# A hybrid two-layer decoder trunk: logarithms, scans and the second mixer's preparation moved to earlier places

## The chip, the cores and the metric

The kernel runs on one core of one Trainium2 chip. The metric is the device time of one execution in microseconds (us). Engines: TensorE (PE) multiplies, VectorE (DVE) and ScalarE (ACT) do elementwise work, SyncE (SP) issues the DMAs. Each engine works through its own instructions in order and waits on semaphores.

## The reference, cut to what matters

Two layers over 256 tokens of width 1024, all float32:

```python
h = rmsnorm(x); p = h @ W_in            # 3592 columns, four head groups
A = hgrn2(...)        # gated linear recurrence, 4 heads x 64, log_f = log of a gate, cumulated
B = gated_deltanet(...)  # conv, l2norm, (I + lower)^-1 by chunks
C = rglru(...)        # associative scan over 256 channels
D = rwkv7(...)        # generalised delta state update
x = x + concat(A, B, C, D) @ W_out
x = x + cross_attention(rmsnorm(x), rmsnorm(mem))     # 256 memory tokens, keys and values from mem
x = x + swiglu(rmsnorm(x))              # layer 0; layer 1: top 2 of 8 experts
```

## The kernel before, in words

Activations stay in SBUF. A weight chunk of 1 MB (128 x 2048 floats) comes by DMA into one of three `raw` buffers; ACT rounds it to `whi` (L447), DVE makes the rest `wlo = raw - whi` (L871, L1318), and PE multiplies in three passes (hi*hi, lo*hi, hi*lo). `plan_chunks` lists the order of loads, and the ring of three `raw` buffers means that load d starts when chunk d - 3 is used up. `ahead(n)` on ACT and DVE splits chunks up to n at that point of the engine's program.

A layer runs so:

1. Input projection: 14 chunks, `cm_phase` on PE, evacuated by ACT (`cm_evac`) with a hook `gates_ahead(l, j)` ahead of chunk j on each engine.
2. `gates(l)` and `logs(l)`: lora products, sigmoids, the logarithms of the decays.
3. `hgrn(l)`: the cumulated decay by four scans, then LEVELS = 7 levels. At level v ACT makes an exponential, DVE two products `H` ("hg_qk"), PE the scores, DVE takes them over (`take`) and makes the differences of level v + 2 (`diff`). Between these stand steps of the RG-LRU (`rglru(l, v)`). Behind the levels: the state, the outputs and the preparation of the delta mixer (norms of q and k, decays `gd_cum`, `rel`).
4. `deltanet(l)`: a triangular inverse in seven levels (`inverse`, DVE and PE in turn, "first inverse" here), with parts of RWKV between, then a tail of two solves, a state and the outputs. On DVE it is preceded by `head_out`, the gated norm of the HGRN output.
5. `rwkv(l)`: masks, a second `inverse`, a tail, then the first products with `w_out`.
6. `attention(l)`: norm, query product, scores, output product.

The keys and values of the memory do not depend on x. Their eight pieces `kv(l, i)` of 16 products each (plain float32, straight out of `raw`) are spread over steps 3 to 5 on PE as filler; `KV_BANK` gives their PSUM banks and `kv_put` their evacuation by ACT. A `w_out` part on PE is `tm_part`, and `tm_add` on DVE adds the result to x.

Of the kernel before, what the change touches and what calls it, by code (L numbers as in the profile page):

```python
# [14 lines left out]
P = 128  # L15
D = 1024
# [6 lines left out]
NH = 4  # L23
# [59 lines left out]
def plan_chunks():  # L83

    out = []
    for layer in range(DEPTH):
        out += [("cm", "w_in", layer, c) for c in W_IN_COLS]
        out += [("tm", "w_out", layer, TM_ROWS * j) for j in range(3)]
        out += [("kv", "xattn_wk", layer, c) for c in range(0, D, CM_COLS)]
        out += [("kv", "xattn_wv", layer, c) for c in range(0, D, CM_COLS)]  # L90
        out += [("tm", "w_out", layer, 3 * TM_ROWS)]
        out += [("cm", "xattn_wq", layer, c) for c in range(0, D, CM_COLS)]
        out += [("tm", "xattn_wo", layer, r) for r in range(0, KT, TM_ROWS)]
        if layer == 0:
            steps = D_FF // CM_COLS
            for j in range(steps + 1):
                if j < steps:
                    out += [("cm", "ffn_w_gate", 0, CM_COLS * j), ("cm", "ffn_w_up", 0, CM_COLS * j)]
                if j:
                    out += [("tm", "ffn_w_down", 0, TM_ROWS * (j - 1))]  # L100
    return out


def build(nc, A, out):
# [14 lines left out]
    with ExitStack() as ctx:  # L119
# [14 lines left out]
        x = sb("x", TT * D)[:, :].rearrange("p (t n) -> p t n", t=TT)  # L134
        hT = [sb(f"hT_{s}", KT * SEQ, F32R)[:, :].rearrange("p (c n) -> p c n", c=KT) for s in ("hi", "lo")]
        def shared(name, cols, before, dt=F32):
            return nc.alloc_sbuf_tensor_at(name, [P, cols], dt, offset=nc.sbuf_base - before)

        hE_flat = [sb(f"hE_{s}", KT * SEQ, F32R) for s in ("hi", "lo")]
# [100 lines left out]
        G_N = H(7), H(13)  # L240
# [120 lines left out]
        KV_BANK = [7, 5, 6, 7, 6, 7, 7, 2]  # L361
# [67 lines left out]
        def _(act):  # L429
# [35 lines left out]
            def cm_evac(n0, count, dst, scale=1.0, after=None):  # L465
                for j in range(count):
# [3 lines left out]
                    ahead(n + SPL)  # L470
# [15 lines left out]
            def kv_put(l, i):  # L486

                bank, j = KV_BANK[i], i % NH
# [6 lines left out]
            def gates_ahead(l, j):  # L495
# [17 lines left out]
                if j == 11:  # L513
                    act.wait_ge(S("shift"), l + 1)
                    a(PT[0:64, D_W * SEQ:(D_W + 1) * SEQ], PT[0:64, D_W * SEQ:(D_W + 1) * SEQ], ACT.Tanh)
                    a(pt(D_G, 1), pt(D_G, 1), ACT.Sigmoid).then_inc(S("lora_in"), 1)
                    a(tmp(0), pt(A_F), ACT.Sigmoid, scale=-1.0).then_inc(S("s_kA"), 1)
                    a(tmp(1), pt(A_G), ACT.Sigmoid)
                if j == 12:
                    a(tmp(2), pt(B_Z), ACT.Sigmoid).then_inc(S("s_z"), 1)  # L520
                    if l:
                        a(tmp(5), pt(A_F), ACT.Sigmoid)
                if j == 13:
                    act.wait_ge(S("gelu_in"), l + 1)
                    a(tmp(4), tmp(4), ACT.Sigmoid).then_inc(S("gelu_s"), 1)

            def gates(l):

                ahead(first_chunk["w_out", l] + SPL)
                act.wait_ge(S("lora_mm"), l + 1)  # L530
                for j in range(2):
                    a(pt(C_X)[:, 256 * j:256 * j + 256], ps[:, 2, 256 * j:256 * j + 256], ACT.Sigmoid, bias=pc("rwkv_w0", l, j))
                for j in range(2):
                    a(pt(D_W)[:, 256 * j:256 * j + 256], ps[:, 3, 256 * j:256 * j + 256], ACT.Sigmoid, bias=pc("rwkv_a0", l, j))
                a(H(12), ps[:, 4, :], ACT.Copy).then_inc(S("lora_s"), 1)
                if l:
                    act.wait_ge(S("vmix_mm"), 1)
                    a(H(13)[0:32, 0:256], ps[0:32, 5, 0:256], ACT.Copy).then_inc(S("vmix1"), 1)
                    act.wait_ge(S("vmix_mm"), 2)
                    for j in range(2):  # L540
                        a(tmp(3)[:, 256 * j:256 * j + 256], ps[:, 6, 256 * j:256 * j + 256], ACT.Sigmoid,
                          bias=pc("rwkv_v0", None, j)).then_inc(S("vmix2"), 1)

            def logs(l):

                o, o2 = PCOL["gdn_A_log", l][0], PCOL["lru_lambda", l][0]
                table("exp_and_others")
                act.wait_ge(S("gd_x"), l + 1)
                a(col(ST_SP, 8), col(ST_X, 8), ACT.Abs)
                a(col(ST_LAM, 2), par[:, o2:o2 + 2], ACT.Abs)  # L550
                if l == 0:
                    a(tmp(5), pt(A_F), ACT.Abs)
                    a(tmp(5), tmp(5), ACT.Exp, scale=-1.0)
                a(col(ST_SP, 8), col(ST_SP, 8), ACT.Exp, scale=-1.0)
                a(col(ST_EXPA, 4), par[:, o:o + 4], ACT.Exp)
                a(col(ST_LAM, 2), col(ST_LAM, 2), ACT.Exp, scale=-1.0)
                if l == 0:
                    a(tmp(5), tmp(5), ACT.Ln, bias=1.0).then_inc(S("hg_ln"), 1)
                else:
# [3 lines left out]
                a(col(ST_LAM, 2), col(ST_LAM, 2), ACT.Ln, bias=1.0).then_inc(S("lam_sp"), 1)  # L563
                table("exp_and_others")

            def rglru(l, v):

                if v == 1:
                    act.wait_ge(S("lru_log"), l + 1)
                    a(H(10), H(8), ACT.Exp)  # L570
                    a(H(11), H(8), ACT.Exp, scale=2.0).then_inc(S("lru_a"), 1)
                if v == LEVELS - 1:
                    act.wait_ge(S("lru_gain"), l + 1)
                    a(G_N[0], pt(B_Q), ACT.Square)
                    a(G_N[1], pt(B_K), ACT.Square).then_inc(S("gd_sq"), 1)

            def hgrn(l):
                for v in range(LEVELS):
# [5 lines left out]
                    if v % 2 == 0 and v < LEVELS - 1:  # L584
                        kv_put(l, v // 2)
                    rglru(l, v)
                act.wait_ge(S("hg_qk"), (l + 1) * LEVELS)
                a(tmp(6), pt(A_F), ACT.Exp)
                for c in range(2):
                    b = pt(A_F)[:, 256 * c:256 * c + P]  # L590
                    a(tmp(7)[:, P * c:P * c + P], b, ACT.Exp, scale=-1.0, bias=b[:, P - 1:P]).then_inc(S("hg_end"), 1)
                table("natural_log")
                a(H(11), H(11), ACT.Ln)
                kv_put(l, 3)
                act.wait_ge(S("gd_ss"), l + 1)
                for j in range(2):
                    a(G_N[j], ps[:, j, :], ACT.Ln, bias=epsc(0))
                act.wait_ge(S("hg_trk"), l + 1)
                a(tmp(5)[:, 0:256], ps[:, 5, 0:256], ACT.Copy).then_inc(S("hg_kd"), 1)
                a(H(11), H(11), ACT.Exp, scale=0.5).then_inc(S("lru_root"), 1)  # L600
                for j in range(2):
                    a(G_N[j], G_N[j], ACT.Exp, scale=-0.5).then_inc(S("gd_rn"), 1)
                act.wait_ge(S("gd_gd"), l + 1)
                a(col(ST_GD, 8), col(ST_GD, 8), ACT.Exp)
                act.wait_ge(S("gd_cum"), 3 * l + 3)
                a(tmp(2), ps[:, 4, :], ACT.Exp).then_inc(S("gd_eg"), 1)
                for p_ in range(2):
# [1702 lines left out]
```

## Time and profile before

| | us |
|---|---|
| median of 3 runs | 1986.95 (1986.77 to 1990.31) |
| the profiled execution | 1990.8 |
| its span | 1989.0 |
| PE busy | 1873.3 (94%) |
| DVE busy | 1466.7 (74%) |
| ACT busy | 1131.7 (57%) |

The share of busy time is an average over stages with different limits. The mixers (steps 2 to 5) of layer 0 lie between 109 and 288 us, those of layer 1 between 675 and 857 us; the experts fill the time from 975 us to the end.

### The profile page before, as it was taken

The page shows a single profiled execution, that of the slowest core. Times are in us where ns is not written, and L with a number is a line of the kernel's source. Part 1 is how long each engine was busy: PE and PEld are TensorE (multiplying, and loading weights), DVE is VectorE, ACT ScalarE, POOL GpSimd, SP SyncE. Part 2 cuts the span into 40 slices and gives each one's busy share as a digit, 9 for nine tenths or more (in the row PEclk, how much of TensorE's full clock was granted, in tenths as well). Part 3 has the DMA queues.
Part 4 walks back from the last instruction along what each step waited for, and adds up shares of the span by engine and source line. Part 5 has one row for each costly group of instructions (what it writes and reads, how often), then busy time and mean ns, then how long its engine had stood idle before and what let it go on. Part 6 is the DMA issues. An engine that isn't in the chain of part 4 may idle for free.

```text
span 1989.0 us, 29716 instructions
## 1 busy us (share of the span) xinstructions
PE 1873.3 (94%) x12520; PEld 1617.3 (81%) x12521; DVE 1466.7 (74%) x1547; ACT 1131.7 (57%) x1065; POOL 0.2 (0%) x4
## 2 busy tenths in 40 slices
PE   7998799999999988899699999999999999999996
PEld 6976688899989877778588888888888888888885
DVE  6767645444457677553698989989899898998985
ACT  5555224443344652143377767777677777777774
POOL 0000000000000000000000000000000000000000
PEclk9998899999999999899799999999999999999998
DMA  7541004255545421023499999999999999999992
GB/s 239 171 149 59 28 23 162 85 191 182 182 145 170 157 78 44 23 92 118 161 345 341 381 345 366 370 330 379 346 369 367 330 380 346 370 365 333 377 374 97
DMA packets 239450, 465.99 MB, mean 234 GB/s; under 512 B 11856, under 2 KB 87760, under 8 KB 239312
## 3 DMA queue, kind: packets, MB, share of 16 engines
q1 hardware_dynamic: 239312, 464.03, 65.6%
q8 instruction: 101, 1.65, 0.3%
q14 instruction: 37, 0.30, 0.0%
HBM read 462.95 MB, written 1.05 MB: 233 GB/s over the span
## 4 chain that ended last, share of the span: by engine, by line
PE 84%; DVE 10%; ACT 3%; issue 2%; DMA 0%; DVEq 0%; SPq 0%; ACTq 0%
PE ps L2077 31%; PE ps L1557 15%; PE ps L2087 15%; PE ps L1542 11%; PE ps L1577 6%; DVE MT L858 4%; PE ps L2133 2%; PE ps L1622 1%; PE ps L2108 1%; ACT MT L438 1%; DVE MT L861 1%; PE ps L2148 1%; DVE MT L864 1%; DVE x L858 1%; DVE TMP L858 1%
## 5 line engine op out<-in xcount | busy, mean ns | idle before, releaser
L1318 DVE TENSOR_TENSOR wlo<-raw,whi 128x2048 fp32r<-128x2048 f32 x140 | 320.4, 2291 | 55.7 <-ACT whi L736 55.5
L736 ACT ACTIVATE whi<-raw 128x2048 fp32r<-128x2048 f32 x140 | 268.9, 1922 | 120.8 <-PE ps L2087 71.2
L871 DVE TENSOR_TENSOR wlo<-raw,whi 128x2048 fp32r<-128x2048 f32 x85 | 194.5, 2289 | 98.9 <-ACT whi L447 98.7
L1318 DVE TENSOR_TENSOR wlo<-PT,whi 128x2048 fp32r<-128x2048 f32 x84 | 192.1, 2292 | 31.2 <-ACT whi L736 30.2
L447 ACT ACTIVATE whi<-raw 128x2048 fp32r<-128x2048 f32 x85 | 162.1, 1907 | 45.2 <-PE ps L1577 43.6
L2077 PE MATMUL ps<-whi,hE_hi 128*128 128x512 f32 x672 | 185.4, 398 | 2.4 <-DVE hE_lo L1387 2.4
L736 ACT ACTIVATE whi<-PT 128x2048 fp32r<-128x2048 f32 x84 | 161.4, 1922 | 34.9 <-PE ps L2077 34.2
L2077 PE MATMUL ps<-wlo,hE_hi 128*128 128x512 f32 x672 | 180.1, 390 | 0.0
L2077 PE MATMUL ps<-whi,hE_lo 128*128 128x512 f32 x672 | 179.8, 389 | 0.0
L2077 PEld LDWEIGHTS ps<-wlo,hE_hi 128*128 128x128 f32 x672 | 126.2, 188 | 27.2
L2077 PEld LDWEIGHTS ps<-whi,hE_lo 128*128 128x128 f32 x672 | 126.1, 188 | 26.7
L2077 PEld LDWEIGHTS ps<-whi,hE_hi 128*128 128x128 f32 x672 | 122.0, 188 | 24.8 <-DVE hE_lo L1387 2.6
L2087 PE MATMUL ps<-whi,act_hi 128*128 128x512 f32 x336 | 130.8, 389 | 1.4 <-DVE act_lo L1362 1.4
L2087 PE MATMUL ps<-whi,act_lo 128*128 128x512 f32 x336 | 130.8, 389 | 0.0
L2087 PE MATMUL ps<-wlo,act_hi 128*128 128x512 f32 x336 | 130.7, 389 | 0.0
L1542 PE MATMUL ps<-MT 64*64 64x64 f32 (+1 forms) x2528 | 98.9, 233 | 26.4 <-DVE MT L858 18.8
L1542 PEld LDWEIGHTS ps<-MT 64*64 64x64 f32 (+1 forms) x2528 | 90.4, 146 | 38.4 <-issue 19.2
L1557 PE MATMUL ps<-hT_hi,whi 128*128 128x256 f32 x848 | 119.7, 284 | 0.0
L1557 PE MATMUL ps<-hT_hi,wlo 128*128 128x256 f32 x848 | 119.0, 283 | 0.0
L1557 PE MATMUL ps<-hT_lo,whi 128*128 128x256 f32 x848 | 119.0, 283 | 0.0
L858 DVE TENSOR_TENSOR MT<-MT,ps 128x256 f32<-128x256 f32 (+2 forms) x99 | 44.6, 450 | 90.2 <-PE ps L1557 75.5
L1557 PEld LDWEIGHTS ps<-hT_hi,whi 128*128 128x128 f32 x848 | 109.9, 192 | 0.9
(272 smaller groups left out, 3397.5 us busy)
## 6 DMA issues: line engine op xcount, KB each, us to landing
raw<-in_moe_w_up SPq DMA_DIRECT2D x111, 1024.0 KB, 6.8
PT<-in_moe_w_down SPq DMA_DIRECT2D x56, 1024.0 KB, 6.4
PT<-in_moe_w_gate SPq DMA_DIRECT2D x55, 1024.0 KB, 6.7
TMP<-in_moe_w_gate SPq DMA_DIRECT2D x55, 1024.0 KB, 6.6
raw<-in_moe_w_down SPq DMA_DIRECT2D x55, 1024.0 KB, 6.0
raw<-in_w_in SPq DMA_DIRECT2D x28, 1024.0 KB, 5.4
raw<-in_ffn_w_gate SPq DMA_DIRECT2D x11, 1024.0 KB, 5.3
raw<-in_ffn_w_up SPq DMA_DIRECT2D x11, 1024.0 KB, 5.5
```

What stands on the lines that cost most here:

```text
L438: return chain.link(lambda: nc.scalar.activation(o, i, f, **kw))
L447: nc.scalar.activation(whi[i % SPL][:, :], raw[d % RAW][:, :], ACT.Copy).then_inc(S("w_hi"), 1)
L736: nc.scalar.activation(ex_hi[m % XSPL], ex_raw[m % XRAW], ACT.Copy).then_inc(S("w_hi"), 1)
L858: return chain.link(lambda: V.tensor_tensor(o, x0, x1, op))
L871: V.tensor_tensor(wlo[i % SPL][:, :], raw[d % RAW][:, :], whi[i % SPL][:, :].bitcast(F32), ALU.subtract).then_inc(S("w_lo"), 1)
L1318: V.tensor_tensor(ex_lo[m % XSPL], ex_raw[m % XRAW], ex_hi[m % XSPL].bitcast(F32), ALU.subtract).then_inc(S("w_lo"), 1)
L1542: return Signalled(pe.matmul(o, lhsT, rhs, start=start, stop=stop, skip_group_check=True))
L1557: ins = pe.matmul(ps[:, bank, SEQ * m:SEQ * m + SEQ], wp[a_][:, k, P * m:P * m + P], src[b_][:, k, :], start=i == 0 and k == 0, stop=last)
L1577: ins = pe.matmul(ps[:, 4 + 2 * t + hf, :], src(b_, kk, t), wp[a_][:, kk, 512 * hf:512 * hf + 512], start=first and kk == 0 and i == 0, st ...
L2077: ins = pe.matmul(ps[:, bank, :], h_[b_][:, X_K * i + k, :], wp[a_][:, k, :], start=i == 0 and n_ == 0 and k == 0, stop=i == 1 and n_ == 2 ...
L2087: ins = pe.matmul(ps[:, 4 + hf, :], act_[b_][:, P * (TM_ROWS * i + kk):P * (TM_ROWS * i + kk) + P], wp[a_][:, kk, 512 * hf:512 * hf + 512] ...
L2133: ins = pe.matmul(g_tokens(c), xs[:, t, P * c:P * c + P], oneh[:, P * t:P * t + P], start=t == 0, stop=t == 1)
```

## The change

Nothing is computed differently but for the form of one polynomial; work changes its place, and some intermediate results lie in buffers of the weight split (`spare`) that are free in the mixers.

- The lora products, the logarithms, the four scans and the first two differences are hooks of the projection's chunks 10 to 12. So are the products for the norms of the delta mixer's q and k.
- `second(v)` puts the delta mixer's preparation and the HGRN state into the seven levels, on PE and DVE.
- The last RG-LRU step and the HGRN `head_out` stand in levels 4 and 2 of the first inverse.
- The eight `kv` pieces have other places, the last one in `attention`, half of it (PRE = 4 of 8) ahead of the norm; the load order follows.
- The `w_out` chunks 0 to 2 are split in the mixers' tails instead of right behind the projection.
- `tm_add` asks for one split less before it adds; `norm` asks for it.

```diff
@@ plan_chunks
-        out += [("tm", "w_out", layer, TM_ROWS * j) for j in range(3)]
-        out += [("kv", "xattn_wk", layer, c) for c in range(0, D, CM_COLS)]
-        out += [("kv", "xattn_wv", layer, c) for c in range(0, D, CM_COLS)]
-        out += [("tm", "w_out", layer, 3 * TM_ROWS)]
+        out += pieces[0:4] + w_out[0:1] + pieces[4:6] + w_out[1:2] + pieces[6:7] + w_out[2:4] + pieces[7:8]
@@ scalar
-                if j == 11:
+                if j == 10:
...
+                if j == 12:
...
+                    logs(l)
+            def gates_late(l, j):
+                if j != 11:
+                    return
+                act.wait_ge(S("lora_mm"), l + 1)
...
+                a(G_N[0], pt(B_Q), ACT.Square)
+                a(G_N[1], pt(B_K), ACT.Square).then_inc(S("gd_sq"), 1)
@@ vector
+                def second(v):
+                    if v == 0:
...
+                        stt(pt(B_Q), pt(B_Q), HD ** -0.5, G_N[0], ALU.mult, ALU.mult)
+                    if v == 1:
+                        tt(pt(B_K), pt(B_K), G_N[1], ALU.mult)
+                        dve.wait_ge(S("gd_cum"), 4 * l + 2)
+                        tt(g_kb(l), pt(B_K), ps[:, 5, :], ALU.mult).then_inc(S("gd_ops"), 1)
...
+                def beside(v):
+                    rwkv_ahead(l, v)
+                    if v == 2:
+                        head_out(l, 0, 7, tmp(0), lambda c: pc("hgrn_norm", l, c), pt(A_G), 0)
+                    if v == 4:
+                        rglru(l, LEVELS)
+                inverse(2 * l, after=beside)
...
+                ahead(first_chunk["w_out", l] + 1)
@@ tensor
+            def second(l, v):
+                if v == 0:
+                    pe.wait_ge(S("hg_v"), l + 1)
...
+                if v in (2, 3):
...
+                            mm(ps[:, 4, a_:a_ + P], col(k).to_broadcast([P, P]), incl).then_inc(S("gd_cum"), 1 if t and c else 0)
...
-                kv(l, 0, range(KT))
+                kv(l, 0, range(KT // 2))
...
+                    if v < 5:
+                        kv(l, (v + 1) // 2, range(KT // 2) if v % 2 else range(KT // 2, KT))
@@ deltanet, rwkv_ahead(v)
-                    if v < 2:
-                        kv(l, 5, range(KT // 2 * v, KT // 2 * v + KT // 2))
+                    if v >= 3:
+                        pe.wait_ge(S("y_put"), 4 * l + 1)
+                        kv(l, 3, range(2 * v - 6, 2 * v - 4))
@@ rwkv, turn_operands(v)
+                    kv(l, 5, [v, v + 1] if v == LEVELS - 1 else [v])
@@ attention
+                kv(l, 7, range(PRE))
                 pe.wait_ge(S("x_done"), 6 * l + 2)
                 norm(2 + 3 * l)
+                kv(l, 7, range(PRE, KT))
```

PE, layer 0, from the end of the input projection to the second level. The rows with `sw` are the lora products, those with `memT` the `kv` pieces, `64x64` the scores, `128x8` the sums of the delta mixer's decay. Before:

```order
L1542 MATMUL ps<-PT,sw 128x256 x6
L1545 MATMUL ps<-con,PT 128x128 x4
L1542 MATMUL ps<-memT,raw 128x256 x16
L1542 MATMUL ps<-PT,TMP 64x64 x16
L1542 MATMUL ps<-st,con 128x8
L1542 MATMUL ps<-st 128x8
L1542 MATMUL ps<-memT,raw 128x256 x8
L1542 MATMUL ps<-MT 64x64 x16
L1542 MATMUL ps<-memT,raw 128x256 x8
```

The same place in the changed kernel, where line 1602 is the old 1542:

```order
L1605 MATMUL ps<-con,PT 128x128 x4
L1602 MATMUL ps<-PT,TMP 64x64 x16
L1602 MATMUL ps<-memT,raw 128x256 x8
L1602 MATMUL ps<-st,con 128x8
L1602 MATMUL ps<-st 128x8
L1602 MATMUL ps<-MT 64x64 x16
L1602 MATMUL ps<-con,TMP 128x128 x8
L1602 MATMUL ps<-memT,raw 128x256 x8
```

The lora products are gone from here (they stand in the projection), one piece and a half ahead of level 0 became half a piece, and level 0 has eight products of `second`.

DVE, first inverse, levels 2 to 4 of the changed kernel (`ps,con16b` x2 starts a level, `MT<-MT,ps` x4 ends it; `spare_hi_49` are the RG-LRU's tiles):

```order
L907 TENSOR_TENSOR MT<-ps,con16b 128x256 x2
L907 TENSOR_TENSOR TMP<-ps,TMP 128x512
L913 SCALAR_TENSOR_TENSOR TMP<-TMP,par,PT 128x256 x2
L1125 CAST hT_hi<-TMP 128x512
L907 TENSOR_TENSOR hT_lo<-TMP,hT_hi 128x512
L907 TENSOR_TENSOR MT<-MT,ps 128x256 x4
L907 TENSOR_TENSOR MT<-ps,con16b 128x256 x2
L907 TENSOR_TENSOR MT<-MT,PT 128x512 x2
L907 TENSOR_TENSOR MT<-MT,ps 128x256 x4
L907 TENSOR_TENSOR MT<-ps,con16b 128x256 x2
L907 TENSOR_TENSOR spare_hi_49<-spare_hi_49 128x512
L1118 SCALAR_TENSOR_TENSOR spare_hi_49<-spare_hi_49 128x256 x2
```

Before, levels 2 to 4 held only this:

```order
L858 TENSOR_TENSOR MT<-ps,con16b 128x256 x2
L858 TENSOR_TENSOR MT<-MT,ps 128x256 x4
L858 TENSOR_TENSOR MT<-ps,con16b 128x256 x2
L858 TENSOR_TENSOR MT<-MT,PT 128x512 x2
L858 TENSOR_TENSOR MT<-MT,ps 128x256 x4
L858 TENSOR_TENSOR MT<-ps,con16b 128x256 x2
L858 TENSOR_TENSOR MT<-MT,ps 128x256 x4
```

So `head_out` (five rows' worth) and the last RG-LRU step moved from ahead of the inverse into it.

## Rows read from the trace of the kernel before

**Rows 1.** The page: the chain that ended last, by engine.

```profile
PE 84%; DVE 10%; ACT 3%; issue 2%; DMA 0%; DVEq 0%; SPq 0%; ACTq 0%
```

**Rows 2.** Busy time by stretch, layer 0: us, busy of each engine, clock, DMA share.

```profile
109.00:122.50 13.50, 10.10 (x44) 7.91 (x44) 6.42 (x14) 12.07 (x20) 0.00 (x0) 0.87 0.45 155
122.50:151.50 29.00, 28.53 (x332) 23.07 (x330) 25.83 (x55) 9.34 (x16) 0.00 (x0) 1.00 0.33 110
151.50:187.00 35.50, 27.29 (x247) 21.75 (x246) 26.16 (x45) 20.65 (x32) 0.00 (x0) 0.90 0.19 60
187.00:214.00 27.00, 22.27 (x485) 19.93 (x486) 20.14 (x45) 11.34 (x23) 0.00 (x0) 0.94 0.12 41
266.00:288.00 22.00, 21.99 (x161) 17.75 (x162) 3.04 (x6) 3.37 (x7) 0.00 (x0) 1.00 0.14 48
```

**Rows 3.** The chain of waits in order of time: start, us, what.

```profile
109.25 0.61 ACT PT L438
127.61 0.46 DVE MT L858
215.69 14.05 PE ps L1542 x82
...
674.80 0.61 ACT PT L438
695.61 0.44 DVE MT L858
782.77 13.82 PE ps L1542 x82
```

**Rows 4.** Timeline of ACT in `logs`: start, us, engine, line, what.

```profile
114.78 1.28 ACT L435 ACT_TABLE_LOAD   x1
116.07 0.21 ACT L438 ACTIVATE st<-st 128x8 f32<-128x8 f32 x1
```

**Rows 5.** Timeline of PE: lora, scores, half piece, norms, decays, outputs.

```profile
109.90 2.19 PE L1542 MATMUL ps<-PT,sw 64*128 64x256 f32 x12 [0.69 <-ACT PT L438]
...
129.26 0.69 PE L1542 MATMUL ps<-MT 64*64 64x64 f32 x32
129.88 3.72 PE L1542 MATMUL ps<-memT,raw 128*128 128x256 f32 x16
...
152.34 1.98 PE L1542 MATMUL ps<-MT,con 128*128 128x512 f32 x4 [0.15 <-DVE MT L1094]
...
158.25 1.95 PE L1542 MATMUL ps<-con,TMP 128*128 128x128 f32 x16
160.04 1.84 PE L1542 MATMUL ps<-MT,TMP 128*128 128x128 f32 x36
```

**Rows 6.** Timeline of DVE behind the levels: a plain product, the RG-LRU scans.

```profile
163.20 0.69 DVE L858 TENSOR_TENSOR TMP<-PT,ps 128x512 f32<-128x512 f32 x1
...
165.44 1.42 DVE L1058 TENSOR_TENSOR_SCAN MT<-MT 128x256 f32<-128x256 f32 x2
```

**Rows 7.** Timeline of DVE, first inverse: starts of levels 0, 2, 4 and 5.

```profile
180.26 0.42 DVE L858 TENSOR_TENSOR MT<-ps,con16b 128x256 f32<-128x256 f32 x1
...
195.87 0.95 DVE L858 TENSOR_TENSOR MT<-ps,con16b 128x256 f32<-128x256 f32 x2 [2.34 <-PE ps L1542]
...
204.31 0.95 DVE L858 TENSOR_TENSOR MT<-ps,con16b 128x256 f32<-128x256 f32 x2
...
207.70 0.95 DVE L858 TENSOR_TENSOR MT<-ps,con16b 128x256 f32<-128x256 f32 x2
```

**Rows 8.** Timeline of PE, second inverse: two levels' products.

```profile
246.11 4.25 PE L1542 MATMUL ps<-MT 64*64 64x64 f32 x96 [0.87 <-DVE MT L858]
...
250.60 3.02 PE L1542 MATMUL ps<-MT 64*64 64x64 f32 x96 [0.23 <-DVE MT L858]
```

**Rows 9.** Attention's start: the PE row of the norm, then its stretch.

```profile
311.14 6.67 PE L1542 MATMUL ps<-TMP,x 128*128 128x128 f32 x32 [3.23 <-DVE TMP L861]
...
311.00:314.00 3.00, 2.86 (x13) 2.89 (x14) 1.04 (x5) 1.49 (x2) 0.00 (x0) 0.50 0.59 243
```

More of the change, by code:

```diff
@@ L521, in gates_ahead @@
                     if l:
[L522 to L529, printed above, removed]
-                act.wait_ge(S("lora_mm"), l + 1)
[L531 to L535, printed above, removed]
+                        act.wait_ge(S("vmix_mm"), 2)
@@ L536, in gates @@
                 if l:
                     act.wait_ge(S("vmix_mm"), 1)
[L538 to L542, printed above, removed]
+                    a(H(13)[0:32, 0:256], ps[0:32, 7, 0:256], ACT.Copy).then_inc(S("vmix1"), 1)
@@ L592, in hgrn @@
-                table("natural_log")
[L593 to L602, printed above, removed]
@@ L832, in _ @@
                 table("sigmoid_and_others")
-                cm_evac(first_chunk["w_in", l], 14, lambda j: pt(W_IN_PARTS[j]), after=lambda j: gates_ahead(l, j))
-                act.wait_ge(S("sw_in"), 16 * (l + 1))
-                gates(l)
-                logs(l)
+                cm_evac(first_chunk["w_in", l], 14, lambda j: pt(W_IN_PARTS[j]), after=lambda j: gates_ahead(l, j),
+                        upto=first_chunk["w_out", l], late=lambda j: gates_late(l, j))
                 hgrn(l)
@@ L890, in stats, with norm @@
                         stt(dst[:, t, :], src[:, t, :], col(t), gain, ALU.mult, ALU.mult).then_inc(S("x_done"), 1)
-            def norm(i, gain, dst):
-                ahead(2)
+            def norm(i, gain, dst, upto):
+                ahead(upto)
                 for c in HI_DVE:
@@ L1015, in logs @@
                     stt(tmp(6), pt(A_F), 0.0, tmp(5), ALU.min, ALU.subtract)
+                b = pt(A_F)
+                for i in range(4):
+                    s_ = slice(P * i, P * i + P)
+                    chain.link(lambda: V.tensor_tensor_scan(b[:, s_], ones, tmp(6)[:, s_], 0.0, ALU.mult, ALU.add)).then_inc(S("hg_b"), 1 if i == 3 else 0)
+                diff(l, 0)
+                diff(l, 1)
                 dve.wait_ge(S("gd_sp"), l + 1)
@@ L1243, in deltanet @@
                 rwkv_operands(l)
-                head_out(l, 1, 0, lambda c: pc("gdn_norm", l), pt(B_Z), 1)
+                ahead(first_chunk["w_out", l] + 1)
+                head_out(l, 1, 0, tmp(7), lambda c: pc("gdn_norm", l), pt(B_Z), 1)
             def rwkv(l):
@@ L1255, in rwkv @@
                 inverse(2 * l + 1)
+                ahead(first_chunk["w_out", l] + 2)
                 dve.wait_ge(S("state"), 3 * l + 3)
@@ L1262, in rwkv @@
                 tt(tmp(2), ps[:, 3, :], pt(D_V), ALU.mult)
+                ahead(first_chunk["w_out", l] + 3)
                 dve.wait_ge(S("rk_gn"), l + 1)
@@ L1519, in _ @@
                     stats(MEM_NORM, mem, mem)
-                cm_steps(first_chunk["w_in", l], 14, after=lambda j: gates_ahead(l, j))
-                gates(l)
-                logs(l)
+                cm_steps(first_chunk["w_in", l], 14, after=lambda j: gates_ahead(l, j), upto=first_chunk["w_out", l])
                 hgrn(l)
```

579 lines of the change are left out of this document (312 added, 267 removed).

## The prediction, made before the changed kernel ran

> **What bounds the kernel now.** I read the page's chain first: PE carries 84% of it and DVE 10% [rows 1], so a gain must come from time in which PE waits, or runs slowly, on the chain. The table of busy time by stretch shows where that is. Behind the input projection of layer 0 PE is busy 10.1 of 13.5 us, in the levels 28.5 of 29, behind them 27.3 of 35.5 at a granted clock of 0.90, in the first inverse 22.3 of 27, in the last tail 22.0 of 22 [rows 2]. The sum of PE's idle time between 109 and 214 us is 3.4 + 0.5 + 8.2 + 4.7 = 17 us per layer; anything beyond that must come from a faster clock or from work taken out of this part. Then the chain in order of time gives three marks per layer: the end of the projection (109.25 and 674.80), the first product of level 0 (127.61 and 695.61), and the first solve behind the first inverse (215.69 and 782.77) [rows 3]. Between the first two marks lie 18.4 and 20.8 us, between the last two 88.1 and 87.1 us. I build the same marks for the changed kernel.
>
> **Step 1: the projection takes in `gates` and `logs`.** PE now has the lora products inside it (2.2 us) and the two 512-wide norm products (2.0 us) [rows 5]; layer 1 adds four small ones, which I put at half the lora row each pair, 2.2 us. So the projection ends at 109.25 + 4.2 = 113.4, in layer 1 at 674.8 + 6.4 = 681.2. What was behind it on ACT and DVE (two tables, a logarithm, four scans, two differences) is ready by then if ACT keeps up: PE's hook of chunk 12 waits for ACT's `gd_sq`, and adding up ACT's work from chunk 10 on it comes some 0.2 us ahead of PE. A chunk is 5.8 us, so ACT, which does 12 us of work between chunks 12 and 14, hides. After the last evacuation (0.6 us) and one exponential (0.6 us) level 0 starts: 114.6 and 682.4. Saved: 13.0 and 13.2, together **26.2 us**. Bounds: nothing beyond PE's added 4.2 us if all hides; if ACT comes late at chunk 12 by the length of its tables and logs (10 us in all), half of it is lost.
>
> One check on that. A table load takes 1.28 us and the next activation starts at its end (114.78 + 1.28 = 116.06, and it starts at 116.07) [rows 4]; the changed hook has three such loads. The Trainium skill ("ScalarE: Activation LUTs", section "What ACT_TABLE_LOAD costs") adds a drain, for 2.66 us per switch. By that the three loads would be 4.1 us longer and the evacuation of chunk 12 would come behind PE's last product, which would give back some 2 us per layer. The trace has no such gap, and I go by the trace.
>
> **Step 2: the levels.** Before, a level was 4.3 us: scores 0.6 and half a `kv` piece 3.7 [rows 5], and PE was full. It stays so. Counted from the first product of level 0 (t = 0): PE still has the first half piece and the decay sums, until 4.4; level 0 is scores 0.6 + eight products 1.95 + 3.7 = 6.3 (to 10.7); level 1 4.4 (15.1); levels 2 and 3 with four products each 5.35 (25.8); level 4 4.8 (30.6). DVE gets eight operations of 0.69 or more [rows 6] and needs only some 31.5 us for all seven levels, so it hides in PE's wait but for the end. ACT evacuates piece 2 ahead of the last exponential: level 6 starts at 31.9, and the last `take` ends at 35.1. Before, it was some 26 (from 127.61 to the end of the stretch at 151.5 [rows 2, 3], and a last `take` of 2), so the levels are 9 us longer. Behind them PE has only scores, outputs (1.84) [rows 5], scores, six turns and the inverse's first products: DVE starts the first inverse at 41.0. Before it was 180.26 - 127.61 = 52.7 [rows 3, 7]. Saved 11.7. The stall behind the levels (ACT's eight relus, exponentials and table loads, with PE idle and then at the half clock) is gone, and a `kv` piece of 7.4 us left the path.
>
> **Step 3: the first inverse.** Before, 180.26 to 215.69: 35.4 us. A plain level is 207.70 - 204.31 = 3.4, of which DVE is busy 2.95 [rows 7]; what is put on DVE there counts nearly in full. Levels 0 and 1 lose their `kv` halves, and with them DVE's wait of 2.3 us [rows 7]: level 2 starts 13.4 behind level 0. Level 2 gets `head_out` (0.7 + 1.0 + 0.4 + 0.7 = 2.9): 6.0 instead of 3.8. Level 3 gets a quarter piece (1.85) on PE between two products: 5.4 instead of 4.7. Level 4 gets the RG-LRU's end, 1.42 of scans and four operations (4.1 in all) [rows 6]: 7.3 instead of 3.4. The rest is 8.0 as before plus 1.3 for the quarter ahead of the solve. Sum 13.4 + 6.0 + 5.4 + 7.3 + 9.3 = 41.4. And PE now idles at the start of this inverse as it did at the start of the second, where 96 products took 4.25 us instead of 3.02 because PE had fallen to half its clock [rows 8]: 1.1 us more. So from level 0 of `hgrn` to the solve 41.0 + 42.5 = 83.5, against 88.1 and 87.1. Saved 4.6 and 3.6: **8.2 us**. Bounds: 12 us if the clock holds and the quarter pieces hide; nothing if three more levels of each inverse run at half clock.
>
> **Step 4: the second inverse and its tail.** Each of its levels gets an eighth of a piece, 0.93 us, where PE goes straight from one product to the next; with DVE's slack of 0.3 a level grows by 0.7 in levels 1 to 4, less 0.5 for four turns that moved out: +2.5 us. The tail of 22.0 us is PE's alone [rows 2]; it holds eight eighths instead of six (+1.9) and the four turns (+0.5). Twice 4.9: **-9.8 us**. The splits of `w_out` in the tails (2.29 on DVE, 1.9 on ACT) find DVE and ACT idle there (busy 3.0 and 3.4 of 22 us in the last tail [rows 2]) and are free; without that cover each would cost 2.3. PE's `w_out` products run without a hole before and after.
>
> **Step 5: attention.** Before, PE waited 3.2 us for the norm's diagonal and then did it in 6.67 us, beginning at the half clock (granted 0.50) [rows 9]. Half a piece now fills the gap (3.7, of which 0.5 sticks out). Then the norm finds PE warm: 32 records of 0.12 are 3.9 us, 2.8 less. The other half piece, 3.7, is on the path, and the first product, whose operands are now all there, gives back 0.2. Net +1.2 per layer: **-2.4 us**. Bounds: -8 in all if the clock is low all the same, +3 if the second half hides too. The earlier additions in `tm_add` are worth under 0.3 us each, since the second of them waits for PE's last product in any case; I count none.
>
> **The sum.** 26.2 + 8.2 - 9.8 - 2.4 = 22.2 us. It is made against the profiled execution: span 1989.0 becomes 1966.8. The execution took 1.8 us more than its span and 3.9 more than the median of the runs; 22.2 off that median of 1986.95 gives **1964.8 us**.
>
> **Rivals.**
> *More gain.* PE stays at full clock through the mixers, since the pieces are now in the inverses: no 1.1 us in step 3, the first tail's half-clock stretch and the second inverse's start go too (some 3 us per layer), and the eighths hide. That is 22 + 10 = 32 us, 1955. For it: the pieces fill exactly the holes. Against: level 0 and 1 of the first inverse lost theirs.
> *Half the gain.* The waits come back elsewhere: ACT is late at chunk 12 (3 us per layer), and the load order bites. The third `xattn_wq` chunk can only be fetched when the last `kv` piece is used up, in attention; by my count it is split 1.5 us ahead of its product. A fetch 4 us slower, and both, cost 12 us: 1977. For it: the margins of 0.2 and 1.5 us are thin. Against: PE waits there for nothing that grows with them.
> *The change does not do what it says.* The logarithms hide, but PE in the levels is the bound, so what left steps 2 and 3 returns as filler and only PE's clock and idle time count: gain under 4 us, 1985. Against it: one piece of 7.4 us truly leaves, and step 1 was idle time.
> *Slower.* The clock. DVE-bound levels leave PE idle, it falls to the half clock, a level costs 1.1 us more [rows 8] and the pieces in it double (0.9 to 1.85 more). With 24 such levels in four inverses that is 24 x 1.1 + 16 = 42 us: 1965 + 42 = 2007, and it decides from about 13 levels on. Against: only two or three levels of an inverse showed it, right after a stretch without products.
>
> **How the numbers follow.** My forecast has 0.55, more gain 0.15, half the gain 0.21, no effect 0.04, slower 0.05. A measurement of this kernel tells about 0.2% (4 us) from no change. So faster 0.91, same 0.04, slower 0.05. The forecast's own range is 1958 to 1971 by the bounds of steps 3 and 5; for 8 in 10 I reach to both neighbours: 1952 to 1977.
>
> **What would show it.** Right: the first product of level 0 comes some 5.4 us after the old end of the projection; the last `take` 35 us later; the first inverse starts 41 us after level 0 and takes over 40; the last tail is 24 us instead of 22; the norm in attention takes 4 us. Wrong: PE waiting for ACT ahead of chunk 12, a granted clock of 0.50 over more than three levels of an inverse, or PE waiting for `wlo` at the third query chunk.

## The result, and the profile after

The changed kernel takes 1962.06 us (median of 4 runs, 1961.31 to 1963.1) where the kernel before, timed beside it, takes 1988.63 (4 runs, 1986.77 to 1990.42): a ratio of 0.9863, 95% interval 0.9851 to 0.9875, or 26.6 us less. The profiled span went from 1989.0 to 1959.5 us, by 29.5: the trace of the kernel before is of an execution of 1990.8 us, that of the changed kernel of one of 1961.3. Forecast were 1964.8 us, in a range of 1952 to 1977.

The chain that ended last, by engine, answers to [rows 1]: ACT's 3% became 1%, PE's 84% became 88%.

```profile
PE 88%; DVE 9%; issue 1%; ACT 1%; DMA 1%; DVEq 0%; SPq 0%; ACTq 0%
```

Busy time by stretch in layer 0, as in [rows 2]: the levels, the first inverse, the first tail, the second inverse, the last tail.

```profile
115.26:150.20 34.94, 32.29 (x362) 27.46 (x362) 29.61 (x56) 15.97 (x29) 0.00 (x0) 1.00 0.30 93
...
156.10:198.30 42.20, 31.31 (x547) 26.44 (x546) 33.94 (x73) 15.23 (x27) 0.00 (x0) 0.88 0.01 2
198.36:219.40 21.04, 18.14 (x159) 14.31 (x158) 13.99 (x20) 8.24 (x10) 0.00 (x0) 1.00 0.47 150
219.40:250.81 31.41, 27.57 (x572) 24.01 (x572) 20.23 (x46) 0.60 (x1) 0.00 (x0) 0.95 0.01 3
250.81:268.93 18.12, 18.12 (x142) 15.26 (x141) 3.13 (x3) 3.33 (x7) 0.00 (x0) 1.00 0.31 117
```

The last tail is PE's alone, as before. The first tail now runs at a granted clock of 1.00 (2.4 GHz; 0.50 is 1.2 GHz, and a value between is a mix of the two). The same stretch of the kernel before, from PE's first solve to its start of the second inverse, by the same view:

```profile
215.69:239.45 23.76, 20.86 (x158) 16.54 (x158) 11.78 (x19) 5.85 (x8) 0.00 (x0) 0.88 0.13 45
```

The marks of [rows 3], from the chain in order of time (the projection's last eviction) and DVE's timeline (level 0's first product, layers 0 and 1):

```profile
113.91 0.61 ACT PT L471
...
666.63 0.61 ACT PT L471
```

```profile
115.26 0.43 DVE L907 TENSOR_TENSOR MT<-TMP 128x256 f32<-128x256 f32 x1 [0.24 <-ACT TMP L471]
...
667.98 0.43 DVE L907 TENSOR_TENSOR MT<-TMP 128x256 f32<-128x256 f32 x1 [4.99 <-ACT TMP L471]
```

From last eviction to level 0 it is 1.35 us in both layers; it was 18.4 and 20.8. The two traces, mark by mark (start of layer 1's projection; DVE's first product of level 0; PE's start of the solve, of the second inverse, of `w_out`; the end of the first query product), give where the 29.5 us of the profiled spans went:

| step | forecast, us | measured, us |
|---|---|---|
| 1: projection takes in gates and logs | -26.2 | -25.8 (12.35 and 13.5) |
| 2 and 3: level 0 to the solve | -8.2 | -8.8 (88.1 to 83.1; 87.2 to 83.3) |
| first tail | none | -5.2 (23.8 to 21.0; 23.5 to 21.0) |
| 4: second inverse and last tail | +9.8 | +10.7 (5.9 and 4.9) |
| 5: `w_out` to the end of the first query product | +2.4 | +1.3 (0.2 and 1.1) |
| the rest (feed-forward, layer 1's first norm, the experts) | none | -1.7 |

In the rest, layer 1's first norm works the other way: it took 5.47 us and takes 6.75 (the row of the kernel before; the other stands with e12).

```profile
583.14 5.47 PE L1542 MATMUL ps<-TMP,x 128*128 128x128 f32 x32 [3.14 <-DVE TMP L861]
```

The attention's start answers to [rows 9]. Timeline of PE: half a piece, norm, half a piece.

```profile
293.56 3.61 PE L1602 MATMUL ps<-raw,memT 128*128 128x256 f32 x16
297.01 3.73 PE L1602 MATMUL ps<-TMP,x 128*128 128x128 f32 x32
300.58 3.62 PE L1602 MATMUL ps<-raw,memT 128*128 128x256 f32 x16
```

### The profile page after: what moved, and what is told of

Read it like the earlier page. It is cut to its first block, busy times and chain, and to the rows that moved or that the text cites. A ratio compares the mean times of both kernels' runs of the same rounds, so it can differ in the third digit from the quotient of the medians.

```text
span 1959.5 us, 29713 instructions
## 1 busy us (share of the span) xinstructions
PE 1861.4 (95%) x12520; PEld 1605.6 (82%) x12521; DVE 1465.5 (75%) x1543; ACT 1121.3 (57%) x1057; POOL 0.2 (0%) x4
## 4 chain that ended last, share of the span: by engine, by line
PE 88%; DVE 9%; issue 1%; ACT 1%; DMA 1%; DVEq 0%; SPq 0%; ACTq 0%
PE ps L2148 31%; PE ps L1617 16%; PE ps L2158 16%; PE ps L1602 12%; PE ps L1637 8%; DVE MT L907 2%; PE ps L2204 2%; PE ps L2179 1%; PE ps L1682 1%; PE ps L2219 1%; DVE MT L913 1%; DVE TMP L907 1%; DVE MT L910 1%; DMA raw<-in_w_in 1%; DVE spare_hi L907 0%
## 5 line engine op out<-in xcount | busy, mean ns | idle before, releaser
L787 ACT ACTIVATE whi<-PT 128x2048 fp32r<-128x2048 f32 x84 | 161.5, 1922 | 34.9 <-PE ps L2148 34.2
L1602 PE MATMUL ps<-MT 64*64 64x64 f32 (+1 forms) x2528 | 104.1, 236 | 35.5 <-DVE MT L907 30.8
```

The source lines that it names most:

```text
L787: nc.scalar.activation(ex_hi[m % XSPL], ex_raw[m % XRAW], ACT.Copy).then_inc(S("w_hi"), 1)
L1602: return Signalled(pe.matmul(o, lhsT, rhs, start=start, stop=stop, skip_group_check=True))
```

## Experiments

Each run is compared with the kernel before, timed beside it on the same chip; against its ratio stands the changed kernel's 0.9863 (0.9851 to 0.9875). The changed kernel itself was not timed again beside these runs, which were made on three chips, so between medians a few us apart the ratios decide. By them e2, e4, e10 and e11 are not told apart from the changed kernel, and what they show is read from their traces. The kernels of e2, e3, e4 and e15 leave out seven of the eight pairs of matmuls of a `kv` piece (e2: of three pieces), so their keys or values are incomplete; they show where time goes and compute something else.

| run | median us | ratio to before (95%) |
|---|---|---|
| e1_logs_behind | 1980.62 | 0.9954 (0.9941 to 0.9968) |
| e2_levels_no_kv | 1962.03 | 0.9857 (0.9842 to 0.9872) |
| e3_inv2_no_kv | 1953.77 | 0.9813 (0.9799 to 0.9826) |
| e4_inv1_no_kv | 1965.5 | 0.9867 (0.9852 to 0.9883) |
| e5_pre0 | 1971.78 | 0.9904 (0.9888 to 0.9919) |
| e8_one_set | 1955.6 | 0.9828 (0.9814 to 0.9842) |
| e10_pool | 1964.91 | 0.9868 (0.9852 to 0.9883) |
| e11_both | 1959.92 | 0.9838 (0.9825 to 0.9852) |
| e12_fill_norms | 1953.87 | 0.9823 (0.9802 to 0.9843) |
| e13_fill_inv | 1953.02 | 0.9816 (0.9796 to 0.9837) |
| e15_tail_no_kv | 1955.45 | 0.9819 (0.9806 to 0.9833) |

### e1: the logarithms behind the projection again

```diff
@@ gates_ahead, chunk 12, ScalarE and VectorE alike
-                    logs(l)
@@ behind cm_evac(...) and cm_steps(...) of w_in
+                logs(l)
```

> The changed kernel, with the one call of the logarithms and scans taken from chunk 12 of the input projection and put behind chunk 13, on ScalarE and VectorE alike; gates, norms' squares and everything else stay where the change put them. Theory A (the prediction's step 1: hiding this call is what brings level 0 forward): ScalarE's part is the 11.3 us from 101.79 to 113.10 of the changed kernel's trace, VectorE's scans wait for the first logarithm in it, so level 0's first product goes from 1.3 us behind the last eviction to about 13 us behind it in layer 0 (115.26 to some 127) and, with fewer small rows, some 10 us later in layer 1: 1983 us, about 21 above the changed kernel's 1962. Theory B (the gain of step 1 comes from the gates that moved, and the logarithms would be covered by the chain's other work behind the projection): level 0 later by under 4 us a layer, 1962 to 1970 us.

Measured: 1980.6, 18.6 us above the changed kernel. ACT's timeline, behind the last eviction, and DVE's first product of level 0:

```profile
113.93 0.60 ACT L471 ACTIVATE PT<-ps 128x512 f32<-128x512 f32 x1 [5.16 <-PE ps L1617]
114.55 1.28 ACT L468 ACT_TABLE_LOAD   x1
...
120.40 0.63 ACT L471 ACTIVATE TMP<-TMP 128x512 f32<-128x512 f32 x1
...
124.55 1.29 ACT L471 ACTIVATE MT<-MT 128x512 f32<-128x512 f32 x2
...
127.89 0.42 DVE L907 TENSOR_TENSOR MT<-TMP 128x256 f32<-128x256 f32 x1
```

Level 0's first product starts at 127.89 in layer 0 (the kernel before: 127.61) and 9.4 us behind the last eviction in layer 1. So this one call is 12.6 us of layer 0 and 8.1 of layer 1, 20.7 of step 1's 25.8. Theory A holds. In layer 0 the moved gates alone bring nothing to this mark, and the logarithms decide; in layer 1 the other 5 us come from the gates.

### e2, e10: which engine binds the levels

```diff
+                ks = [k for k in ks if k not in LEFT.get(i, ())]   # kv(l, i, ks); pieces 0, 1, 2: range(7)
```

> The changed kernel without seven of the eight rows of matmul pairs of each of the key pieces 0 to 2, which stand in the seven levels of the first mixer's second part (six half pieces of 3.72 us a layer, of which only the last two matmuls of each piece stay): the keys are not complete. Theory A (VectorE binds the levels: 29.6 us busy of 35.0, its rows 0.03 to 0.1 us apart): the levels become 33 to 34 us long instead of 34.9, although TensorE loses about 19 of its 32 us there. Theory B (TensorE binds them, as the prediction's term had it): they fall to about VectorE's bare 29.6 us or a little more, 4 to 5 us less a layer. In both, TensorE is then idle for half of the stretch, and the granted clock may fall to 0.50 behind it, which the first inverse's rows would show (4.25 instead of 3.02 us for 96 products), 2 to 5 us a layer back. A: 1960 to 1968 us; B: 1952 to 1960 us.

Measured: 1962.0, no change, and levels of theory A's length. The levels by the table of busy time:

```profile
115.32:148.86 33.54, 18.22 (x276) 15.28 (x278) 29.54 (x56) 15.96 (x29) 0.00 (x0) 0.77 0.31 96
```

With 14 us less of PE work there the levels are only 1.4 us shorter. DVE's timeline says where the 1.4 us lie. The copy that waits for PE's decay sums, and the start of the last level, in the changed kernel and then in e2:

```profile
119.29 0.17 DVE L1150 COPY st<-ps 128x16 f32<-128x16 f32 x1 [1.43 <-PE ps L1602]
...
146.72 0.42 DVE L907 TENSOR_TENSOR MT<-TMP 128x256 f32<-128x256 f32 x1
```

```profile
118.03 0.17 DVE L1151 COPY st<-ps 128x16 f32<-128x16 f32 x1
...
145.38 0.42 DVE L908 TENSOR_TENSOR MT<-TMP 128x256 f32<-128x256 f32 x1
```

The one wait of 1.43 us, for the half piece ahead of the decay sums, is gone. From that copy to the last level it is 27.4 us in both (27.43 and 27.35), with PE full in the one and half idle in the other: DVE's own chain has that length, and PE's pieces do not add to it. Of the 1.4 us, 1.1 are given back behind the levels, where PE now comes at a lower clock: from level 0 to the first inverse's first product on PE it is 38.4 us (115.32 to 153.76) against 38.75 in the changed kernel (115.26 to 154.01). The second run was to take DVE's work away instead:

```diff
-                if v == 1:                       # VectorE, rglru: six instructions in levels 1 to 3
-                    ts(ex, la, -1.0 / 120, ALU.mult)
...
+            la, ex = H(7), H(13)                 # GpSimd
+                ts(ex, la, -1.0 / 120, ALU.mult, -1.0 / 24, ALU.add)
+                for c in (-1.0 / 6, -0.5, -1.0):
+                    tt(ex, ex, la, ALU.mult)
+                    ts(ex, ex, c, ALU.add)
```

> The changed kernel with the polynomial of the RG-LRU gain (six instructions of 128x512, 3.6 us of VectorE a layer in levels 1 to 3: 0.43 + 4 x 0.69 + 0.43) given to GpSimd as nine simple instructions, level 4's step waiting for them. Theory A (VectorE binds the levels, as the run without key pieces showed: 33.5 us with 19 us less of TensorE work): the levels get shorter until TensorE's 32.3 busy us bind, 2 to 2.6 us a layer, 1957 us. Theory B (GpSimd's passes slow VectorE's, or take so long that level 4 waits for them): the levels are as long or longer, 1962 to 1972 us.

Measured: 1964.9, 2.9 above by the median, not told apart by the ratio: theory B. Timeline of PE, the scores of levels 3 to 5 in the changed kernel, then in e10:

```profile
134.68 0.69 PE L1602 MATMUL ps<-MT 64*64 64x64 f32 x32
...
139.85 0.69 PE L1602 MATMUL ps<-MT 64*64 64x64 f32 x32
...
144.46 0.69 PE L1602 MATMUL ps<-MT 64*64 64x64 f32 x32
```

```profile
134.22 0.69 PE L1617 MATMUL ps<-MT 64*64 64x64 f32 x32
...
139.38 0.69 PE L1617 MATMUL ps<-MT 64*64 64x64 f32 x32
...
144.26 0.69 PE L1617 MATMUL ps<-MT 64*64 64x64 f32 x32 [0.36 <-DVE MT L930]
```

The steps are 5.17 and 5.16 us to level 4, because PE works there without a hole in both kernels. At level 5 PE has to wait 0.36 us for DVE in e10. This does not say which engine sets the end of the levels, since e10 did not make DVE's chain shorter. Timeline of GpSimd, then of DVE beside it:

```profile
121.62 1.32 POOL L909 TENSOR_TENSOR MT<-MT 128x512 f32<-128x512 f32 x1
```

```profile
121.85 1.38 DVE L930 TENSOR_TENSOR MT<-PT,TMP 128x256 f32<-128x256 f32 x1
...
131.40 1.56 DVE L930 TENSOR_TENSOR spare_lo<-PT,TMP 128x512 f32<-128x512 f32 x1
```

The same rows take 0.43 and 0.69 us where GpSimd is idle. So DVE was busy for as long as before in these levels (29.8 us in the 34.94 us behind level 0's start, against 29.61), though 3.6 us of its work were gone. DVE was never relieved, and what a shorter chain on DVE would bring is open. What the two runs show is a balance: PE is full from the projection's end to level 5, and DVE's chain, with one wait of 1.43 us in it, ends the levels. In the changed kernel, too, PE waits 1.86 us for DVE ahead of the last level's scores:

```profile
147.65 0.68 PE L1602 MATMUL ps<-MT 64*64 64x64 f32 x16 [1.86 <-DVE MT L907]
```

### e3, e15: the pieces in the second inverse and the last tail

> The changed kernel without the eighths of value piece 5 in the second inverse (seven of eight pairs of matmuls left out, 0.93 us each; the values are not complete). Theory A (the second inverse is longer than before because each eighth stands in the chain of its level: 4.37 us a level instead of 3.39): the second inverse falls from 30.6 to about 27 us, the granted clock staying at 1.00 as it was before the change, and the time to about 1955 us. Theory B (the eighths fill idle time and hold the clock): the levels stay at 4.3 us or more, now at a granted clock of 0.50, and the time stays at 1960 to 1964 us.

The edit is e2's, for piece 5. Measured: 1953.8. Busy time of the second inverse, the last tail, and the stretch of layer 1's first norm far behind:

```profile
219.51:247.25 27.74, 21.75 (x548) 20.26 (x549) 20.22 (x46) 0.60 (x1) 0.00 (x0) 0.86 0.01 3
247.25:267.35 20.10, 20.10 (x138) 16.87 (x137) 3.13 (x3) 3.32 (x7) 0.00 (x0) 0.85 0.28 105
561.10:574.70 13.60, 10.73 (x82) 9.66 (x80) 11.15 (x25) 7.61 (x12) 0.00 (x0) 1.00 0.39 120
```

The inverse is 3.7 us shorter (theory A), but its clock falls, and the tail behind it is 2.0 longer: 1.7 net per layer, in both. So the two stretches hold 3.4 of the 8.3 us. Another 3.5 us lie between `w_out` of layer 0 and level 0 of layer 1, where two norms are faster at a higher clock (the feed-forward's takes 3.81 instead of 5.44 us; the last row is the stretch of the other, of which more below). The instructions there are the same, only at another time. In layer 1 the other stretches cancel, and 1.7 us come behind its `w_out`; the traces differ by 6.7 us in all.

> The changed kernel without seven of the eight pairs of matmuls of value piece 6 in the second tail (the values are not complete). Theory A (each pair of 0.95 us fills a wait for ScalarE's copies and holds the clock): the tail gets shorter by no more than 1 us of its 17.95, or longer where the clock falls; 1960 to 1964 us. Theory B (the pairs stand on the chain): the tail falls from 17.95 to 13 to 15 us, 1953 to 1957 us.

The edit is e2's again, for piece 6. Measured: 1955.5. From the last product of the inverse to `w_out`:

```profile
252.45:267.08 14.63, 12.25 (x114) 10.38 (x113) 3.13 (x3) 3.34 (x7) 0.00 (x0) 1.00 0.40 144
```

14.6 instead of 18.1 us in both layers: seven pairs, 5.9 us of PE's busy time, cost 3.5; the rest hides in waits of 0.5 to 0.6 us that come back. Theory B, with the clock at 1.00. So a pair in the tail costs about half its length on average. That is not the price of the two pairs that the change added: they stand at the tail's start and its end, and against the kernel before they cost 0.82 and 0.87 us.

### e4: the quarters in the first inverse

> The changed kernel without the quarters of key piece 3 in the last four levels of the first inverse (seven of eight pairs of matmuls left out; the keys are not complete). Theory A (the quarters hold the granted clock at 1.00 for the tail behind them, which is why the first tail was 22.6 us instead of 25.1): the first inverse gets shorter by 1 to 3 us, the clock falls to 0.50 around the solve, the tail goes back to about 25 us, and the time stays within 2 us of 1962. Theory B (the quarters only cost): the inverse gets 2.5 us shorter a layer, the tail stays at 22.6, 1957 us.

The edit is e2's, for piece 3. Measured: 1965.5, 3.4 above by the median, not told apart by the ratio. The first inverse from PE's first product to the solve, and the first tail; then the same inverse in the changed kernel:

```profile
155.89:200.00 44.11, 29.83 (x553) 25.09 (x552) 35.55 (x77) 15.23 (x27) 0.00 (x0) 0.80 0.01 2
200.00:224.09 24.09, 21.20 (x160) 16.75 (x159) 13.98 (x20) 8.24 (x10) 0.00 (x0) 0.86 0.40 131
```

```profile
154.01:198.36 44.35, 33.46 (x582) 27.75 (x581) 35.76 (x77) 15.23 (x27) 0.00 (x0) 0.88 0.01 2
```

Without the quarters the inverse is 0.2 us shorter, and the tail goes from 21.0 back to 24.1 (layer 1: 0.6 shorter, 22.9). They cost next to nothing and hold the clock of the tail: theory A for the mechanism, though it had 1 to 3 us for the inverse. That is the unforecast gain of 5.2 us. No other run on the changed kernel moves this tail so: it is 21.04 us in both layers of each of them, and 19.77 in those with one table set.

### e5: no piece ahead of the attention's norm

```diff
-        PRE = 4
+        PRE = 0
```

> The changed kernel with all eight pairs of matmuls of the last value piece behind the attention's norm, instead of four ahead of it and four behind it. Theory A (the four pairs ahead fill the 3.2 us in which TensorE would wait for the norm's statistics, and the norm keeps the full clock by them): the norm's 32 matmuls go from 3.73 us back to about 6.7 at a granted clock of 0.50, and of the 3.7 us of matmuls put behind it only a part is covered by the waits ahead of the first query product; 3 to 6 us a layer, 1968 to 1974 us. Theory B (the prediction's: the pairs and their place cost about 1 us a layer and the clock of that stretch doesn't matter): within 2 us of 1962.

Measured: 1971.8, 9.7 above. Timeline of PE:

```profile
296.57 5.44 PE L1602 MATMUL ps<-TMP,x 128*128 128x128 f32 x32 [2.94 <-DVE TMP L910]
301.85 7.07 PE L1602 MATMUL ps<-raw,memT 128*128 128x256 f32 x32
```

The norm takes 5.44 instead of 3.73 us, and all 7.07 us of the piece lie between it and the query product: from the norm's start to that product it is 12.0 us in both layers instead of 6.84, with the norm itself 0.35 us earlier. That is 4.8 us a layer: theory A, with a norm of 5.44 us and not 6.7. The expectation calls theory B the prediction's, but step 5 counted on the warm norm too; its mechanism holds.

### e8, e11: one table set for both functions

```diff
-                table("exp_and_others")
+                table("natural_log_exp_and_others")   # at the head of logs()
...
-                table("natural_log")                  # and the six others of both mixers
```

> The changed kernel with one table set for logarithm and exponential together in both mixers, so that 16 of ScalarE's 32 table loads of 1.28 us go (the logarithms and exponentials then come from that set's fits). Theory A (a load counts where the next engine waits for the exponential behind it: in the first inverse at 168.98 us of the changed kernel's trace and in the first tail at 210.47 us; those at 101 to 112 us are beside the projection, and the one at 275.38 us is beside the output projection): two loads a layer, 5 us, 1957 us. Theory B (also the last tail's counts): 7.7 us, 1954 us. Theory C (the waits are set by VectorE's own work, and a shorter wait turns into another or into a lower granted clock): within 2 us of 1962.

Measured: 1955.6, 6.5 below the changed kernel, with a ratio interval that lies apart from its 0.9851 to 0.9875. ACT's timeline in the first tail, and the tail's row:

```profile
210.24 0.69 ACT L471 ACTIVATE TMP<-ps,st 128x512 f32<-128x512 f32 x1 [1.36 <-PE ps L1596]
210.96 0.63 ACT L471 ACTIVATE TMP<-TMP 128x512 f32<-128x512 f32 x1
```

```profile
198.83:218.60 19.77, 18.08 (x160) 14.31 (x159) 13.99 (x20) 5.67 (x8) 0.00 (x0) 1.00 0.44 147
```

The first tail fell from 21.04 to 19.77 us, by 1.27, in both layers: one load of 1.28 us, no more. That is direct evidence for the price which the prediction took from [rows 4]. The other load on which theory A counted, that of the first inverse, did not bring its 1.28: DVE waited 0.43 us for it in layer 0 of the changed kernel, and the inverse is as long without it (layer 1: 0.9 shorter). So one load a layer is shown, and theory A's 1957 came near for another reason. The Trainium skill ("ScalarE: Activation LUTs", section "What ACT_TABLE_LOAD costs") puts a switch at 2.66 us with its drain; the measurement decides for 1.28. The second inverse and last tail together fell by 1.36 in layer 0, where the inverse's granted clock was 1.00 instead of 0.95, and rose by 0.2 in layer 1, where it was 0.95. About 2 us of the whole came between `w_out` of layer 0 and level 0 of layer 1, with layer 1's first norm at 3.84 instead of 6.75 us.

> The two edits together: one table set for logarithm and exponential, and the polynomial on GpSimd. If both pay, the gains add, since they lie in different stretches (levels; inverse and tails): 1952 us. If GpSimd's passes slow VectorE, the time is that of the table set alone plus what the other run loses.

Measured: 1959.9, 4.3 us above e8, with ratio intervals that overlap. The gains did not add, as the expectation has it for a GpSimd that slows DVE. The first tail is 19.77 us in both layers, as in e8.

### e12, e13: matmuls on constants in PE's waits

```diff
+            def fill(bank, n, c0=0):
+                for _ in range(n):
+                    mm(ps[:, bank, c0:c0 + 256], ident, con[:, 0:256])
@@ ahead of norm(3), of layer 1's first norm and of norm(6)
+                fill(0, 6)
@@ e13 besides: inverse 1, level 1 between its products; behind level 2
+                        fill(2, 5)
+                        fill(0, 4)
```

> The kernel with one table set (e8), with six matmuls of 128x256 on constants (2.8 us, into a bank that nobody reads) put into TensorE's queue where it would wait some 3 us for a norm's statistics: ahead of the feed-forward's norm, of layer 1's first norm, and of the experts' norm. Theory A (a wait of 3 us lets the granted clock fall, and it is the norm behind it that pays: 5.4 to 6.7 us for 32 matmuls instead of 3.73 where the attention's pairs stand ahead): each of the three norms comes to 3.73 us, and what follows them is at full clock too: 5 to 8 us less than e8's 1955.6, so 1948 to 1951 us. Theory B (the clock falls for other reasons, or the filler only takes time): 1955 to 1958 us.

Measured: 1953.9, 1.7 below e8, with intervals that overlap: not told apart, and between the ranges of the two theories. Timeline of PE, layer 1's first norm in the changed kernel, in e3, and in e12:

```profile
567.69 6.75 PE L1602 MATMUL ps<-TMP,x 128*128 128x128 f32 x32 [2.85 <-DVE TMP L910]
```

```profile
564.82 3.84 PE L1603 MATMUL ps<-TMP,x 128*128 128x128 f32 x32 [2.85 <-DVE TMP L911]
```

```profile
560.82 2.75 PE L1596 MATMUL ps<-con 128*128 128x256 f32 x12
563.83 3.84 PE L1596 MATMUL ps<-TMP,x 128*128 128x128 f32 x32 [0.27 <-DVE TMP L904]
```

With the filler all three norms take 3.8 us, where the changed kernel has 5.44, 6.75 and 5.44. But e12 is built on e8, and there the rows of the three norms are these:

```profile
369.82 5.44 PE L1596 MATMUL ps<-TMP,x 128*128 128x128 f32 x32 [2.94 <-DVE TMP L904]
...
565.51 3.84 PE L1596 MATMUL ps<-TMP,x 128*128 128x128 f32 x32 [2.85 <-DVE TMP L904]
...
917.96 3.81 PE L1596 MATMUL ps<-TMP,x 128*128 128x128 f32 x32 [2.94 <-DVE TMP L904]
```

Two of them were fast without filler, behind the same waits. So the filler is shown to do something for the feed-forward's norm alone, 1.6 us. Whether it protects the other two against the slow case, no run here shows.

> As e12, and besides, in the first inverse of each layer, five such matmuls (2.3 us) in level 1 where TensorE waits 2.9 us for VectorE, and four (1.9 us) behind level 2 where it waits 2.2 us. Theory A: the 64 matmuls of level 1 (3.68 us in the changed kernel) and the 96 of level 3 (4.83 us) come to 2.1 and 3.0 us, the stretch from the first inverse's start to the solve gets 1 to 3 us shorter a layer: 2 to 5 us less than e12. Theory B (VectorE binds this stretch, so that the faster matmuls only end in longer waits): within 1 us of e12.

Measured: 1953.0, the same as e12. From PE's first product of the first inverse to the solve it is 44.04 and 44.60 us (e12: 44.19 and 44.22). Theory B. Level 1's 64 products came to 2.08 us (3.68 in e12), and nothing followed from it, since DVE has work of its own there: its takeover of them starts 11.3 us behind its start of the inverse in both. In level 3 DVE waits 0.29 instead of 0.98 us for the faster products, but it had waited 0.69 us for PE, against 0.16, just before. So PE's clock is worth nothing in level 1 and under 1 us in level 3, and this filler brought none of it.

## Why the prediction was right

- **Step 1** was right in mechanism and size, 26.2 against 25.8. It measured 1.35 us from eviction to level 0 (it had said 1.2). What PE got more to do lengthened the projections by 4.7 and 6.0 us (4.2 and 6.4 forecast), without a wait of PE for ACT in either. e1 puts 20.7 of it on the one call.
- **Step 2** gave the marks within 0.2 us: last `take` at 34.9 (35.1), first inverse at 40.8 (41.0). PE was full up to level 5, as it had said. But DVE does not hide in PE's wait: its own chain ends the levels (e2), and PE waits 1.86 us for it. The number held because the two chains, which the step put at 31.9 and some 31.5 us, are that close together; that part is luck.
- **Step 3** named 42.5 us and measured 42.3 and 42.2. In layer 0 its parts 13.4, 6.0, 5.4, 7.3 and 9.3 measured 13.45, 6.5, 5.8, 7.3 and 9.2. The 1.1 us for PE at half clock, which it put beside them, showed only as the 0.4 too much of level 3 (its 96 products took 4.83 us); in level 1 the slow products cost nothing (e13). Level 2's 0.5 hold a wait of 0.43 us of DVE for ACT behind a table load, which the step didn't have.
- **Step 4** forecast 2.5 us for the eighths (its own terms, four times 0.7 less 0.5, give 2.3) and 2.4 for the tail; 3.7 and 2.1 were measured in layer 0, 2.7 and 2.1 in layer 1, where the old inverse had run at a lower clock for longer. The eighths cost a full 0.93 us in each level, since PE had no slack to put them in (4.37 us a level where 3.39 was); e3 shows the same 3.7 from the other side. In the tail the two added pairs cost 1.7 us and the turns 0.4, nearly as counted, although a pair there costs half on average (e15).
- **The step that was missing** is the first tail, 5.2 us. The rival "more gain" named it ("the first tail's half-clock stretch goes too") and was given 0.15; that part of it came true, while its hiding eighths did not. e4 shows that the quarters ahead of the solve do it.
- **Step 5** was near (+1.3 for +2.4), and its cover is real: without it, 9.7 us (e5). The half piece ahead of the norm stuck out by 0.06 us instead of 0.5. The old norm of 6.67 us, from which it took 2.8, stood only in layer 0; in layer 1 it was 5.44, and there the step cost 1.1 us instead of 0.2.
- The time was forecast 2.7 us too high. Of the spans' 29.5 us the sum had 22.2: it missed 5.2 in the first tails, 1.7 in the rest, 1.1 in step 5 and 0.6 in steps 2 and 3, and had 0.4 too much in step 1 and 0.9 too little cost in step 4. (By the medians the gain is 26.6 us, and the kernel before ran 1.7 us slower in this comparison than in the runs the forecast started from.) So the time came out nearer than the gain, by 4.4 us of 26.6 or 7.3 of 29.5, and that is luck. The slower rival did not come: in layer 0 the products ran slowly in levels 1 and 3 of the first inverse and in one level of the second.

## What to carry to other kernels

Count a filler three ways: what it costs in its place (0.93 of 0.93 us where the engine goes straight from one product to the next, half of that on average in a tail of short waits, next to nothing under a waiting engine), what clock it holds for the stretch behind it, and who takes over as the bound when it goes. Before a sum of hidden work is believed, find the chain of the next engine: here 14 us less on PE brought 1.4, and the run that was to relieve DVE only slowed it. Where a logarithm is followed by an exponential on a waited-for path, one table set for both is worth up to a load, and no more than the wait that the load made (1.27 us in the first tail, at most 0.43 in layer 0's first inverse). The best complete kernels run are those with the fillers, 1953.9 and 1953.0; the table set alone has most of it.

## What the runs showed of the hardware

The same wait can be followed by 3 us more or by nothing. Ahead of layer 1's first norm PE waits 2.85 us in the changed kernel, in e3 and in e8; behind it the granted clock was 0.75 over the 13.6 us of the stretch in the first (the norm 6.75 us) and 1.00 in the others (3.84 us), with nothing changed in that stretch but the time at which it came. What decides between the two is open. From the feed-forward's norm to layer 1's first scores it is 295.3 us in the changed kernel and 291.8 in e3 and e12. The way from level 0 to the first inverse in layer 0 varies likewise, from 38.4 to 41.2 us among e2, e4 and the changed kernel, though e4 changed nothing there. Such shifts of 2 to 4 us are as large as the effects of single edits here, which is why the readings above go by stretches of the trace and not by medians alone.

The row of the changed kernel's stretch:

```profile
564.60:578.20 13.60, 10.75 (x67) 10.51 (x66) 9.84 (x22) 6.88 (x12) 0.00 (x0) 0.75 0.33 101
```

GpSimd's passes of 128x512 took 1.3 to 1.8 us beside DVE (the first of them 0.62), and a two-input DVE instruction beside them went from 0.43 to 1.38 and from 0.69 to 1.56 us. The Trainium skill ("GPSIMD Engine Reference", section "Key points") says that the two share their SBUF interfaces, with contention for DVE instructions that have two SBUF inputs. This trace agrees for most rows: `spare_hi<-PT,ps`, whose second input is in PSUM, kept its 0.69 us beside GpSimd (at 126.59). But not every row with two SBUF inputs was slowed (0.42 us at 127.41).
